# One-hot matmuls in place of an index list, a gather and transposes, for the tokens of the first expert in a two-layer hybrid decoder

## What is computed

```python
def moe_swiglu(x, w_router, w1, w3, w2):         # x: 512 tokens x 1024, already RMS-normed and scaled
    logits = jnp.einsum("td,de->te", xf, w_router)   # 8 experts
    top_vals, top_idx = lax.top_k(logits, 2)
    gates = jax.nn.softmax(top_vals, axis=-1)
    ...                                          # group the 1024 (token, expert) pairs by expert
    def expert_block(args):
        xblk, e = args
        h = jax.nn.silu(xblk @ w1[e]) * (xblk @ w3[e])   # 1024 -> 3584
        return h @ w2[e]                                 # 3584 -> 1024
    ...                                          # each token adds its two experts' rows, times its gates
```

## Time and profile before

| | us |
|---|---|
| median of three runs | 2118.0 |
| the three runs | 2118.04, 2118.00, 2115.34 |
| the profiled execution | 2119.46 |
| its span, first to last instruction | 2117.6 |
| TensorE busy in it | 2021.0 (95%) |
| VectorE, ScalarE, GpSimd busy | 1545.5, 1217.9, 90.0 |
| mean granted TensorE clock | 0.982 of full speed |

### The profile page before, as it was taken

The page is one execution under the profiler, slowest core; times in us unless marked ns, Lnnn a source line. Parts: engine busy times, 40 slices in busy tenths (PEclk is TensorE's granted clock), DMA queues, the critical chain, the costliest instruction groups (busy, mean ns, idle before and its releaser), DMA issues.

```text
span 2117.6 us, 33187 instructions
## 1 busy us (share of the span) xinstructions
PE 2021.0 (95%) x10939; PEld 1757.9 (83%) x10940; DVE 1545.5 (73%) x1695; ACT 1217.9 (58%) x1554; POOL 90.0 (4%) x132
## 2 busy tenths in 40 slices
PE   7999999999999996999999999999999999999992
PEld 6777888888897776999999888888998888889991
DVE  6896666666678966665766698897666888986655
ACT  4543555555554434555655577776555777865553
POOL 1000000000000002000000000000000000000002
PEclk9999999999999997999999999999999999999996
DMA  6321766756552225776877699998776999997743
GB/s 204 131 70 56 226 211 214 217 186 188 188 160 100 80 80 168 240 237 198 293 237 238 218 385 353 387 372 320 238 238 200 363 375 363 388 354 238 237 139 133
DMA packets 245441, 488.17 MB, mean 231 GB/s; under 512 B 16724, under 2 KB 86468, under 8 KB 245396
## 3 DMA queue, kind: packets, MB, share of 16 engines
q1 hardware_dynamic: 237668, 462.04, 64.7%
q0 software_dynamic: 7728, 25.52, 3.4%
HBM read 473.20 MB, written 14.30 MB: 230 GB/s over the span
## 4 chain that ended last, share of the span: by engine, by line
PE 80%; DVE 10%; issue 4%; ACT 2%; DMA 2%; POOL 1%; DVEq 0%; POOLq 0%; ACTq 0%; SPq 0%
PE PS L1338 79%; DVE wlo L687 3%; DVE PS L789 2%; DMA raw<-in_expert_w 1%; ACT whi L352 1%; DVE OV L763 1%; DVE OV L777 1%; PE PS L1630 1%; PE PS L1356 0%; DVE OV L793 0%; DMA OV<-in_norm_mix_g 0%; DVE OV L759 0%; DMA OV<-y_rows,addr 0%; DVE OV L710 0%; DVE OV L924 0%
## 5 line engine op out<-in xcount | busy, mean ns | idle before, releaser
L687 DVE TENSOR_TENSOR wlo<-raw,whi 128x1024 fp32r<-128x1024 f32 x882 | 1043.5, 1221 | 208.8 <-ACT whi L352 200.1
L352 ACT ACTIVATE whi<-raw 128x1024 fp32r<-128x1024 f32 x882 | 896.3, 1053 | 230.7 <-PE PS L1338 131.3
L1338 PE MATMUL PS<-XN,whi 128*128 128x352 f32 (+2 forms) x3328 | 984.1, 368 | 15.7 <-DVE OV L924 7.7
L1338 PE MATMUL PS<-XN,wlo 128*128 128x176 f32 (+2 forms) x2944 | 792.5, 269 | 2.0 <-issue 2.0
L1338 PEld LDWEIGHTS PS<-XN,whi 128*128 128x128 f32 x3328 | 623.3, 190 | 80.5 <-issue 12.8
L1338 PE MATMUL PS<-whi,XN 128*128 128x512 f32 x2272 | 669.4, 393 | 8.8 <-DVE XN L798 3.5
L1338 PEld LDWEIGHTS PS<-XN,wlo 128*128 128x128 f32 x2944 | 565.7, 192 | 15.3 <-issue 2.3
L1338 PEld LDWEIGHTS PS<-whi,XN 128*128 128x128 f32 x2272 | 423.6, 188 | 103.3 <-issue 6.9
L1338 PE MATMUL PS<-wlo,XN 128*128 128x512 f32 x1248 | 423.2, 391 | 0.0
L1338 PEld LDWEIGHTS PS<-wlo,XN 128*128 128x128 f32 x1248 | 234.4, 188 | 50.5
L1338 PE MATMUL PS<-whi,hid 128*128 128x512 f32 x384 | 111.6, 392 | 0.8 <-DVE hid L883 0.8
(11 more groups left out here) (197 smaller groups left out, 931.9 us busy)
## 6 DMA issues: line engine op xcount, KB each, us to landing
raw<-in_expert_w SPq DMA_DIRECT2D x672, 512.0 KB, 5.1
raw<-in_ffn_w SPq DMA_DIRECT2D x144, 512.0 KB, 3.5
raw<-in_w_in SPq DMA_DIRECT2D x40, 512.0 KB, 4.9
raw<-in_w_out SPq DMA_DIRECT2D x16, 512.0 KB, 4.3
y_rows<-OV POOLq DMA_DIRECT2D x14, 512.0 KB, 4.9
y_rows<-OV POOLq DMA_DIRECT2D x14, 192.0 KB, 6.1
RES<-in_x SPq DMA_DIRECT2D x4, 512.0 KB, 6.1
x_tok<-OV POOLq DMA_DIRECT2D x4, 512.0 KB, 2.9
```

Source lines behind the costliest of these rows:

```text
L352: act.activation(whi[:, u0 % CONV, half(h)], raw[:, r, half(h)], ACT.Copy).then_inc(s["hi_done"], 1)
L687: dve.tensor_tensor(wlo[:, w, half(h)], raw[:, u0 % RAW, half(h)], whi[:, w, half(h)].bitcast(F32), ALU.subtract).then_inc(s["lo_done"], 1)
L1338: return pe.matmul(out_, lhsT, rhs, start=start, stop=stop, skip_group_check=True)
```

## The change

The first expert's tokens are no longer listed, gathered and transposed. The last norm writes its four blocks into four buffers of their own (`x4`), which stay there; and PE multiplies each of the 8 x 4 blocks of 128 features x 128 tokens with the one-hot map `S0` of that block of tokens (128 x 176), adding over the four blocks. The result has features in partitions and the 176 places in columns, which is what the transposes gave. It fills banks 4 to 7, `f_T(0)` and `f_T(1)` holding four groups of features each, and each half is split by one ScalarE copy and one VectorE subtraction of 128 x 704 numbers. These 32 matmuls are of type float32.

With it go: the wait of VectorE for the list and the two copies into `idx`; the first gather on GpSimd and its waits for buffers of `xt`; the waits of the last norm for `xt` buffers; and the split of unit 2 ahead of the low parts, which now stands behind them with units 3 and 4. VectorE's first subtraction stands behind the addresses, the second behind the table and the gates. The squares of the last norm share one scratch buffer and wait for each other. Expert 1's gather and the later ones are as before.

The diff, cut to its core:

```diff
+        def f_T(h):
+            return PS[:, 4 + 2 * h:6 + 2 * h, 0:2 * WIN].rearrange("p a (k n) -> p a k n", n=WIN)
         def x_home(n):
-            if q == 0:
+            if q in (0, 3):
                 return x4[:, b, :]
...
 # ScalarE
-            x_split(0)
-            x_split_ext(0)
+            for h in range(2):
+                act.wait_ge(s["gT_done"], 1 + h)
+                act.activation(XX[:, 0, 4 * h:4 * h + 4, :], f_T(h), ACT.Copy).then_inc(s["ghi_done"], 1 + h)
...
 # VectorE
+            def first_split(h):
+                dve.wait_ge(s["ghi_done"], 1 + 2 * h)
+                k = slice(4 * h, 4 * h + 4)
+                dve.tensor_tensor(XX[:, 1, k, :], f_T(h), XX[:, 0, k, :].bitcast(F32),
+                                  ALU.subtract).then_inc(s["glo_done"], 1 + h)
...
-            dve.wait_ge(s["first_list"], 1)
-            dve.tensor_copy(idx[:, 0:1], PS[:, 3, 0:1])
-            dve.tensor_copy(idx[0:WIN - P, 1:2], PS[0:WIN - P, 3, 1:2]).then_inc(s["idx_ok"], 1)
...
             ins.then_inc(s["addr_ok"], 1)
+            first_split(0)
...
-            split(MOE_BASE + 2, 0)
-            x_split(0)
-            x_split_ext(0)
-            for i in range(3, LEAD):
+            first_split(1)
+            for i in range(2, LEAD):
                 split(MOE_BASE + i, 0)
+            dve.wait_ge(s["x_stored"], 16 * TB)
...
 # GpSimd
-            gather(0, first=True)
...
 # TensorE
             pe.wait_ge(s["first_sel"], 1)
-            for b in range(TB):
-                mm(PS[:, 3, 0:1], S0[:, b, 0:P], tokf[:, b:b + 1], b == 0, b == TB - 1)
-            for b in range(TB):
-                ins = mm(PS[0:WIN - P, 3, 1:2], S0[:, b, P:WIN], tokf[:, b:b + 1], b == 0, b == TB - 1)
-            ins.then_inc(s["first_list"], 1)
-            gT(0)
-            gT_ext()
+            pe.wait_ge(s["xlo_done"], 4 * TB)
+            for j in range(KD):
+                for b in range(TB):
+                    ins = mm(f_T(j // 4)[:, (j % 4) // 2, j % 2, :], x4[:, b, j * P:(j + 1) * P], S0[:, b, :],
+                             b == 0, b == TB - 1)
+                if j % 4 == 3:
+                    ins.then_inc(s["gT_done"], 1)
             first_windows(pe, visit)
```

More of the change, by code:

```diff
@@ L160, in build_program @@
           y_part y_evac gath_in gT_done ghi_done glo_done y_stored
-          log_done log_sb log_T first_sel first_list gd_ok gate_exp sel_ok pos_done addr_ok list_zero zero_out list_out lists_in idx_ok turns sizes_ok table_ok
+          log_done log_sb log_T first_sel gd_ok gate_exp sel_ok pos_done addr_ok list_zero zero_out list_out lists_in idx_ok turns sizes_ok table_ok
           fin0 fin1 fin2 fin3 fin_acc fin_ready out_done""".split()
@@ L397, in norm @@
                     act.wait_ge(*ready(b))
-                    squares(q * TB + b, junk[:, b % 2, :])
+                    if q == 3 and b:
+                        act.wait_ge(s["ss_done"], q * TB + b)
+                    squares(q * TB + b, OV[:, 5632:6656] if q == 3 else junk[:, b % 2, :])
                     for n in ((), (), (0, 1), (2,))[b]:
@@ L660, in _ @@
             act.wait_ge(s["hid_zero"], 4)
+            act.wait_ge(s["x_stored"], 16 * TB)
             first_windows(act, visit)
@@ L745, in norm @@
                         dve.wait_ge(s["gB_in"], 16 * q)
-                    if b >= 2:
+                    if b >= 2 and q != 3:
                         dve.wait_ge(s["xT_done"], n - 1)
-                        if q == 3:
-                            dve.wait_ge(s["x_stored"], 16 * (b - 1))
                     scaled(n)
@@ L1061, in _ @@
             dve.wait_ge(s["log_T"], 1)
-            dve.wait_ge(s["const_ok"], 4)
+            dve.wait_ge(s["const_ok"], 3)
             def pick(v, m, i, mask):
@@ L1268, in _ @@
                 if b:
-                    if b >= 2:
-                        pool.wait_ge(s["x_stored"], 16 * (b - 1))
                     pool.wait_ge(s["xt_done"], 3 * TB + b)
-                    pool.dma_start(x_tok[(b - 1) * P:b * P, :], xt[:, (b - 1) % 2, :]).then_inc(s["x_stored"], 16)
+                    pool.dma_start(x_tok[(b - 1) * P:b * P, :], x4[:, b - 1, :]).then_inc(s["x_stored"], 16)
             def held(semaphore, value):
@@ L1277, in held, with gather @@
                 pool.sem_inc(s["turns"], 1)
-            def gather(v, first=False):
-                if not first:
-                    held(s["gT_done"], v * 2)
-                    pool.tensor_copy(idx[:, :], lists[:, :, bass.ds(v, 1)].rearrange("p b one -> p (b one)")
-                                     ).then_inc(s["idx_ok"], 1)
-                held(s["idx_ok"], 1 if first else v + 1)
+            def gather(v):
+                held(s["gT_done"], v * 2)
+                pool.tensor_copy(idx[:, :], lists[:, :, bass.ds(v, 1)].rearrange("p b one -> p (b one)")
+                                 ).then_inc(s["idx_ok"], 1)
+                held(s["idx_ok"], v)
                 for n, (a, b) in enumerate(blocks):
@@ L1548, in gT @@
             def gT(i):
-                pe.wait_ge(s["gath_in"], i * 32 + 32)
+                pe.wait_ge(s["gath_in"], i * 32)
                 for k in range(KD):
```

6 lines of the change are left out of this document (2 added, 4 removed).

## The result

The changed kernel took 2122.64 us, the median of 12 runs (2117.05 to 2125.19); the kernel before, run beside it, took 2116.88 (12 runs, 2113.14 to 2118.89). The ratio is 1.0025, with a 95% interval of 1.0017 to 1.0033: 5 to 6 us slower, above the range of 2112.5 to 2120.5. The profiled execution took 2124.94, with a span of 2123.1 against 2117.6 before. So the same file has two levels: the forecast of 2116.0 is what it does on some chips, and the first result is what it does on another.

The account below looks back on a forecast made before the run. TensorE, busy 95%, was taken to bound the kernel. The first visit's lead, 2.3 or 1.3 us by case, was taken as 1.9; 2118.0 - 1.9 gave 2116.0 rounded, range 2112.5 to 2120.5.

Parts of the forecast that it names:

- The float32 matmuls: Added on PE from 802.6: 64 records, 0.295 then 0.148 us apart, full clock after 5.6 us, ending at 814.9.
- The work behind them: ScalarE copy 0.77 us and VectorE subtraction 0.89 us per half, with table and gates, 4.0 us, between the subtractions.
- The second high part is ready at 814.9 + 0.1 + 0.77: ScalarE's second copy done at 815.8, second subtraction 816.0 to 816.9, so PE may begin the visit at 817.0.
- The loads are no later bound: First visit's weights: a load takes 3.8 us; unit 6's second half copied by 826.5, before VectorE needs it at 827.3.
- the supply as forecast: VectorE's ten halves at 1.15 us and one sum, from 816.9, let PE enter the visit's second part at 829.0.
- The branch: PE's jump to unloaded code, 3.85 us, begun around 813.6, ending near 817.4; up to 0.4 us, counted as nothing.
- branch (a): First visit: no stop on "issue"; PE waits 3.3 us for the sum, half clock loses 1.6; lead 2.3 us.
- the rival of an uncovered branch: Visit starts at 819.8, its 32 pairs end at 834.4, 1.5 us late; 2119.5 us in all; chance 0.08.
- The clock: PE's wait before the visit's second part is followed by 3.4 us at half clock, a loss of 1.6 us.
- The sum: Whole kernel: about 1.9 us gained, 2118.0 - 1.9 = 2116.0 rounded, called the same.
- The two branches: First visit without the stop on "issue", lead 2.3 us, or with it, 4.15 us long, lead 1.3 us.
- The slower rival that I priced: Float32 matmuls stay at the low clock, ending at 821.5; 2122 to 2123.5 us; chance 0.08.

Follow-up runs that it names:

- experiment 1: The changed kernel run again, unaltered: 2115.74 us, ratio 0.9993 to the kernel before.
- Experiment 3: The changed kernel with PE's sequencer waiting for both halves of the float32 matmuls before the loop and its branch: 2115.04 us, ratio 0.9986.
- experiment 5: The changed kernel with only unit 2's split moved ahead of the first split of the expert's tokens: 2112.67 us, ratio 0.9971.
- experiment 6: The changed kernel again, unaltered, in another call: 2116.98 us, ratio 0.9995 to the kernel before.
- experiment 17: The changed kernel with the list scatters held until the eighth unit of the first visit is used: 2115.38 us, ratio 0.9993.

## Why the prediction was wrong, point by point

- **The float32 matmuls** held: 0.293 and 0.149 us a record, the clock back after 5.0 us (forecast 5.6), the last record at 814.2 (814.9), the first half at 809.4 (810.1).
- **The work behind them** held in size: copy 0.76 (0.77), subtraction 0.89, table and gates 811.1 to 815.1.
- **"The second high part is ready at 814.9 + 0.1 + 0.77" is the step that failed.** The 0.1 is what was wrong: from a record's end to its signal it was 0.014 us in the median of some 650 in the kernel before, and 4.4 us here, so that ScalarE's copy began at 818.72 and the visit at 820.63 instead of 817.0. The scatters had come to stand beside a matmul that somebody waits for: the prediction had said that `addr_ok` comes earlier and "GpSimd's list work is then earlier too; nobody waits for it". True, nobody waits for it, and yet, as far as the runs tell, it held up a signal.
- **"The loads are no later bound"** failed as well, by its size: the 3.8 us came from one load with nothing beside it. With the next expert's gather beside them halves landed 2.5 to 2.7 us apart, where in experiment 1 all but the first two came 1.3 us apart, and the second part came 15.7 us after the visit's start instead of 12.0. The earlier list work alone does not bring the gather there: in experiment 1 the scatters stand as early, and the loads of units 5 and 6 have landed before the gather at 828.3. The late signal had moved the loads back, and the gather, at 823.6, fell among them. In experiment 1 the term was 12.7: the supply as forecast, within 0.7.
- **The branch** was covered, and the stop on "issue" was gone, as in branch (a). Experiment 3 shows that the rival of an uncovered branch was wrongly priced too: its start is 4 us late, but the wait ahead of the second part and the half clock in it go, and at the end of that part 0.3 us are left.
- **The clock** was right in kind. The Trainium skill (TensorE: Matmul & The Clock Gate, section "HAM oscillation — how this bites in real kernels") says that idle stretches between bursts bring it down; the trace agrees, with 0.50 behind both of PE's waits, and in experiment 5, where the second wait is gone, the second fall is gone. But not every wait did it: behind one of 2.16 us in experiment 6 and one of 1.80 us in experiment 17 the clock stayed at 1.00. I had one fall of 1.6 us in the sum; a later and longer wait made it 2.3.
- **The sum**, 1.9 us gained, was right where its assumption holds: on three chips of the first kind the changed kernel's median lay 1.1 to 1.4 us under that of the kernel before, inside what can be told from no change. (The two branches gave 2.3 and 1.3, whose mean is 1.8, not 1.9; nothing hangs on it.) The slower rival that I priced (clock stays low, 2122 to 2123.5) has the time of the result by luck: the clock did come back in the matmuls, and the time has another mechanism, which I had not thought of.

## What to carry to other kernels

When an edit makes a queue's work start earlier, look up what it will then stand beside, also where no one waits for it: here list scatters and a gather, which nobody in this stage waits for, seem to cost 6 us or more on one kind of chip by standing beside a signal and a row of loads, and nothing that can be measured on the other; holding them back by 45 us cost nothing on either. When a stage has a late start and a late supply, find out which one sets its second part before working on the first: taking list, gather and transposes away gained about 1 us, which can't be told from nothing, and moving one unit's split ahead of a wait that was there anyway gained 4. And measure on more than one chip before believing 0.2%.

## What the runs showed of the hardware

- A matmul's signal can come 3.7 to 4.8 us after its record's end. It was seen in the first result and in five executions on one chip, each time with indirect transfers completing beside it (16 increments each, one transfer every 1.27 us), and followed one of their bursts by 0.3 to 0.4 us. In the kernel before, with such transfers beside it and 292 of their increments recorded, the signals were on time.
- Chips differ in how many of some 337 increments of the transfers' semaphore the trace records: 236 to 311 in the first result and on two chips, 333 to 337 on three others.
- PE's branch to code not yet run took 3.4 to 4.3 us in every kernel, wherever it stood.
- A float32 matmul of 176 columns takes two records, 0.149 us apart at the full clock and 0.293 at half.
